# Fifteen row blocks instead of sixteen for the experts of a mixture-of-experts stage, with pieces of 32, 64 and 128 rows

## The chip, the cores and the metric

The kernel runs on one core of one Trainium2 chip. The metric is the device time of one execution in microseconds (us). The time before is 2076.75 us, the median of three runs (2075.97 to 2078.27 us).

## The reference, cut to what matters

Two layers are computed for 640 tokens of width 1024. Each layer has three mixers that read one input projection, and then a channel mixer: a mixture of 16 experts, of which each token takes two. Only that last part is touched here.

```python
def moe_ffn(h, w_router, router_bias, wg, wu, wd):
    scores = jax.nn.sigmoid(xt @ w_router)
    ...                                    # best group, then its best two experts: eidx (T, 2)
    e_flat = eidx.reshape(-1)              # 640 tokens x 2 = 1280 rows, each for one of 16 experts
    ...                                    # the rows are sorted by expert and padded
    def expert_block(args):
        xblk, e = args
        a = jax.nn.silu(xblk @ wg[e]) * (xblk @ wu[e])     # (rows, 1024) @ (1024, 512), twice
        return a @ wd[e]                                   # (rows, 512) @ (512, 1024)
    ...                                    # each token's two rows are weighted and added
```

Everything is float32. The weights of one expert are three matrices of 2 MB each (gate, up and down), so a layer reads 48 of them.

## The kernel before

**Rows and blocks.** In each layer the kernel counts on the chip how many rows each expert has, and ranks the experts by that count. Rank 0 is the fullest. Each rank has a fixed capacity of rows (`CAPS`) and a fixed first row (`BASES`) in a list of rows that is cut into blocks of 128. With capacities of 256, 256, 192, 192, six times 128 and six times 64 there are `NBK` = 16 blocks. An expert with more rows than its rank's capacity sends the rest to one of `OVB` = 8 overflow blocks, which are computed behind the others, in a loop whose body is skipped where there is nothing to do.

**The order of the blocks.** `RUN` names for each step the block and the two ranks that own its lower and upper 64 rows: four blocks belong to two ranks, twelve to one. `MATS` is the order in which the weights are fetched. For each step in which ranks are new it lists their gate, then their up, then their down matrices. `LAST` is the last step that uses a rank.

**Weights.** There are `NSLOT` = 8 slots of 2 MB in SBUF. Matrix m goes to slot m modulo 8, and the sync engine (SP) issues its fetch (line 449) once matrix m - 8 has been used for the last time (`moe_used`, awaited at line 355). SP issues them strictly in the order of `MATS`. Behind the last of them, SP issues the first three weight blocks of the next layer's input projection.

**One step on TensorE.** The loop is:

```python
for i in range(NBK):
    pe.wait_ge(xT_evac, nth(l, NBK, i + 1))
    hidden(i, 0)              # gate product, 8 k-steps
    if i + 1 < NBK:
        tokens_in(i + 1)      # transposes of the next block's tokens (L843)
    hidden(i, 1)              # up product, 8 k-steps
    if i:
        outputs(i - 1)        # down products of the block before, 2 halves of 4 k-steps
    turn_hidden(i)            # four transposes (L866)
```

All gate, up and down products are made by `product` (line 855). For each k-step and each piece of the block it issues one matmul: the piece's rows of the transposed tokens are the stationary operand (128 x rows), 512 columns of the expert's weights are streamed, and the result goes to the piece's rows of a PSUM bank. The profile has two records for each such float32 matmul, here called two passes. A block of one rank has one piece with 128 columns of TensorE's array. A block of two ranks has two pieces with 64 columns each, which lie beside each other in the array.

**Around it.** GpSimd gathers each block's tokens from DRAM (line 1287). VectorE copies the transposed tokens, multiplies gate and up, and copies one half of the result. ScalarE does the activation, copies the other half, and stores each finished block of results in DRAM.

Of the kernel before, what the change touches and what calls it, by code (L numbers as in the profile page):

```python
# [28 lines left out]
P = 128  # L29
# [30 lines left out]
NE = 16  # L60
# [2 lines left out]

CAPS = [256, 256, 192, 192] + [128] * 6 + [64] * 6
BASES = [sum(CAPS[:i]) for i in range(NE)]
NBK = sum(CAPS) // P
NB = NBK + OVB


RUN = [(7, (4, 4)), (0, (0, 0)), (1, (0, 0)), (13, (10, 11)), (2, (1, 1)), (3, (1, 1)), (14, (12, 13)), (4, (2, 2)),
       (5, (2, 3)), (6, (3, 3)), (15, (14, 15)), (8, (5, 5)), (9, (6, 6)), (10, (7, 7)), (11, (8, 8)), (12, (9, 9))]
NSLOT = 8


def moe_matrices():

    order, last = [], {}
    for i, (_, who) in enumerate(RUN):  # L80
        new = [s for s in sorted(set(who)) if s not in last]
        order += [(s, j) for j in range(3) for s in new]
        for s in who:
            last[s] = i
    return order, last


MATS, LAST = moe_matrices()
MAT = {m: i for i, m in enumerate(MATS)}
NEG = 1e30  # L90
# [27 lines left out]
def nth(l, per, n):  # L118
    return l * per + n
# [12 lines left out]
def build_program(nc, A):  # L132
    with ExitStack() as ctx:
# [3 lines left out]
        def sem(name):  # L137
            return ctx.enter_context(nc.semaphore(name))

        def dram(name, shape):  # L140
            return nc.dram_tensor(name, shape, F32, kind="Internal").ap()
# [5 lines left out]
        x_dram = dram("x_dram", [T, D])  # L147
        exp_dram = dram("exp_dram", [NB * P, D])

# [23 lines left out]
        def view(off, n, pattern=None, **kw):  # L173
            v = ar[:, off:off + n]
            return v.rearrange(pattern, **kw) if pattern else v
# [46 lines left out]
        yb = [view(26624 + 1024 * s, 1024) for s in range(2)]  # L222
# [6 lines left out]
        at_row = view(12288, 10 * P, "p (a r) -> p a r", a=10)  # L229
        at_block = view(12288 + 10 * P, 10 * NB, "p (a b) -> p a b", a=10)  # L230

        def slotA(j):
            return wA[:, j * SLOT:(j + 1) * SLOT]
# [8 lines left out]
        def bank(i, n=512):  # L242
            return psum[:, i * 512:i * 512 + n]
# [9 lines left out]
        def sm(n):  # L253
            o[0] += n
            return small[:, o[0] - n:o[0]]
# [23 lines left out]
        rowf, blkf = sm(10), sm(10)  # L279
        ids = ismall[:, 10:10 + NB]  # L280
        novi = ismall[:, 36:37]
# [53 lines left out]
        xg_in = [sem("xg_in0"), sem("xg_in1")]  # L335
        xT_done, xT_evac = sem("xT_done"), sem("xT_evac")
        gate_done, up_done, sg_ready, a_ready = sem("gate_done"), sem("up_done"), sem("sg_ready"), sem("a_ready")
        aT_done, aT_ready, y_done = sem("aT_done"), sem("aT_ready"), sem("y_done")
        yA_evac, yB_evac = sem("yA_evac"), sem("yB_evac")
        y_stored = [sem("y_stored0"), sem("y_stored1")]  # L340
# [10 lines left out]
        def until(eng, signal, n):  # L351


            eng.wait_ge(signal, n)
            eng.sem_inc(passed[eng.engine], 1)
# [19 lines left out]
        def moe_landed(l, m):  # L375

            s_, n = m % NSLOT, m // NSLOT + 1
            return (landedA[s_], loadsA(l, s_, (3, 2, 4)[s_]) + 16 * n) if s_ < 3 else (landedB[s_ - 3], l * 96 + 16 * n)

        def moe_used(l, m):  # L380

            s_, j = MATS[m]
            return (gate_done, up_done, y_done)[j], (32 if j == 2 else 16) * l + (LAST[s_] + 1) * (2 if j == 2 else 1)

        def s3(v, k=KD):
            return v.rearrange("p (k c) -> p k c", k=k)
# [107 lines left out]
        def _(pe):  # L494
# [19 lines left out]
            for l in range(DEPTH):  # L514
# [103 lines left out]
                for ci, c in enumerate(JOBS):  # L618
# [21 lines left out]
                    for j in range(NL + 1):  # L640
# [11 lines left out]
                        for w in range(NT):  # L652
                            tk = slice(w * P, (w + 1) * P)
                            for h in range(2):
                                r = slice(64 * h, 64 * h + 64)
# [19 lines left out]
                    if dr == 1:  # L675
# [12 lines left out]
                        for w in range(NT):  # L688
                            ent = (0 if w == 0 else 1 + w, 1 if w == 0 else 2 + w)
                            for d_ in range(2):  # L690
                                for h in range(2):
                                    r = slice(64 * h, 64 * h + 64)
# [114 lines left out]
                for t in range(NT):  # L807
                    pe.wait_ge(tr_evac, nth(l, N_TR, 2 * NT + 2 * t + 2))
                    for half in range(2):
# [3 lines left out]
                        w = s3(slotA(SLOT_OF[7 + half]))  # L813
# [14 lines left out]
                for a in range(2 * NT):  # L828
                    mm = pe.matmul(bank(5)[:, 0:NB], at_row[:, a, :], at_block[:, a, :],
                                   start=a == 0, stop=a == 2 * NT - 1)  # L830
# [3 lines left out]
                def tokens_in(i):  # L834

                    p = i % 2
                    pe.wait_ge(xg_in[p], l * 128 + 16 * (i // 2 + 1))
                    if i:
                        pe.wait_ge(xT_evac, nth(l, NBK, i))
                    if i >= 2:  # L840
                        pe.wait_ge(aT_ready, nth(l, NBK, i - 1))
                    for k in range(KD):
                        mm = pe.transpose(psum[:, 3072 + k * P:3072 + (k + 1) * P], xg[p][:, k * P:(k + 1) * P], ident)  # L843
                    mm.then_inc(xT_done, 1)

                def product(out, act_T, i, j, kn, cs):

                    a, b = RUN[i][1]
                    parts = [(a, slice(0, P))] if a == b else [(a, slice(0, 64)), (b, slice(64, P))]
                    for s_, r in parts:  # L850
                        pe.wait_ge(*moe_landed(l, MAT[s_, j]))
                    for k in range(kn):
                        for s_, r in parts:
                            w = s3(moe_slots[MAT[s_, j] % NSLOT], kn)
                            mm = pe.matmul(out[r, :], act_T[:, k, r], w[:, k, cs], start=k == 0, stop=k == kn - 1)  # L855
                    return mm
# [4 lines left out]
                def turn_hidden(i):  # L861
                    pe.wait_ge(a_ready, nth(l, NBK, i + 1))
                    if i + 1 < NBK:
                        pe.wait_ge(xT_evac, nth(l, NBK, i + 2))
                    for q in range(4):
# [64 lines left out]
        def _(act):  # L930
# [18 lines left out]
            for l in range(DEPTH):  # L949
# [45 lines left out]
                for b, dst, fn in ((1, kf, ACT.Sigmoid), (2, qf, ACT.Copy)):  # L995
# [4 lines left out]
                    for c in (range(5) if b == 1 else (0, 4)):  # L1000
                        pb = unit_ready(AT[b, c])
                        if c < 4:
                            a = act.activation(dst[:, c, P:T], pb, fn)
                        else:
                            a = act.activation(dst[:, :, 0:P], pb.rearrange("p (c t) -> p c t", c=4), fn)
# [20 lines left out]
                for ci, c in enumerate(JOBS):  # L1026
                    at = {second: n for n, first, second in UNITS[ci]}
# [9 lines left out]
                    for j in range(NL):  # L1037
# [4 lines left out]
                        if j == 1:  # L1042
# [4 lines left out]
                            a, b = (kfac, qfac) if c < 2 else (qfac, kfac)  # L1047
# [94 lines left out]
                def y_half(i):  # L1142
                    act.wait_ge(y_done, nth(l, 2 * NBK, 2 * i + 2))
                    if i >= 2:
                        act.wait_ge(y_stored[i % 2], l * 128 + 16 * (i // 2))
                    act.activation(yb[i % 2][:, W:D], bank(5), ACT.Copy).then_inc(yB_evac, 1)  # L1146

                def y_store(i):
                    act.wait_ge(yA_evac, nth(l, NBK, i + 1))
                    act.wait_ge(yB_evac, nth(l, NBK, i + 1))  # L1150
                    act.dma_start(exp_dram[RUN[i][0] * P:(RUN[i][0] + 1) * P, :], yb[i % 2]).then_inc(y_stored[i % 2], 16)

                for i in range(NBK):
                    act.wait_ge(gate_done, nth(l, NBK, i + 1))
# [11 lines left out]
                y_half(NBK - 1)  # L1166
                y_store(NBK - 1)

                until(act, y_stored[0], l * 128 + 128)
                until(act, pos_ready, l + 1)  # L1170
                nov = act.value_load(novi[0:1, :], min_val=0, max_val=OVB)
                with act.Fori(0, OVB) as j:
# [17 lines left out]
                for t in range(NT):  # L1190
                    for q in range(2):
                        a = act.activation(by_weight[:, 2 * t + q, :], ident, ACT.Copy, scale=wt[:, t, q:q + 1])
# [8 lines left out]
        def _(gp):  # L1201
            gp.memset(condW[:], 0.0).then_inc(cond_zero, 1)
            gp.memset(mhalf, -0.5)
            for s_ in range(NE):
                gp.memset(table[:, 0, s_:s_ + 1], float(CAPS[s_]))
                gp.memset(table[:, 1, s_:s_ + 1], float(BASES[s_]))
            gp.memset(zeros, 0.0)
# [6 lines left out]
            for l in range(DEPTH):  # L1214
# [66 lines left out]
                until(gp, h_stored[0], l * 48 + 48)  # L1281
                until(gp, h_stored[1], l * 32 + 32)
                until(gp, ids_ready, l + 1)
                for i, (blk, _) in enumerate(RUN):
                    if i >= 2:
                        until(gp, xT_done, nth(l, NBK, i - 1))
                    gp.indirect_dma_start(xg[i % 2], None, tok_dram,  # L1287
                                          bass.IndirectOffsetOnAxis(ap=ids[:, blk:blk + 1], axis=0)).then_inc(xg_in[i % 2], 16)
                until(gp, pos_ready, l + 1)
                until(gp, xT_done, nth(l, NBK, NBK))  # L1290
                nov = gp.value_load(novi[0:1, :], min_val=0, max_val=OVB)
# [10 lines left out]
                        gp.dma_start(spare[0:1, bass.ds(j, 1)], bass.AP(A["router_bias"].tensor, 0, [[1, 1], [1, 1]])).then_inc(ov_g, 16)  # L1302
                until(gp, ov_g, l * (16 * OVB) + 16 * OVB)

                until(gp, y_stored[0], l * 128 + 128)
                until(gp, y_stored[1], l * 128 + 128)
                until(gp, ov_st, l * (16 * OVB) + nov * 16 + 16)

                for t in range(NT):
# [15 lines left out]
        def _(v):  # L1325
# [64 lines left out]
            for l in range(DEPTH):  # L1390
# [355 lines left out]
                for t in range(NT):  # L1746
                    dr_()
                    a = tt(before[:, (t + 1) * NE:(t + 2) * NE], before[:, t * NE:(t + 1) * NE], M[:, t, :], ALU.add)
# [52 lines left out]
                for q, oh in enumerate((oh1, oh2)):  # L1801
# [12 lines left out]
                dr_()  # L1814
                tt(at_block, blkf.unsqueeze(2).to_broadcast([P, 2 * NT, NB]),
                   cst[:, C_IOTA:C_IOTA + NB].unsqueeze(1).to_broadcast([P, 2 * NT, NB]), ALU.is_equal)
                tt(at_row, rowf.unsqueeze(2).to_broadcast([P, 2 * NT, P]),
# [33 lines left out]
                def y_half(i):  # L1851
                    v.wait_ge(y_done, nth(l, 2 * NBK, 2 * i + 1))
                    if i >= 2:
                        v.wait_ge(y_stored[i % 2], l * 128 + 16 * (i // 2))
                    v.tensor_copy(yb[i % 2][:, 0:W], bank(4)).then_inc(yA_evac, 1)

                tokens_out(0)
# [121 lines left out]
```

## Time and profile before

| | |
|---|---|
| median of three runs | 2076.75 us |
| profiled execution | 2085.36 us |
| its span | 2083.5 us |
| busy: TensorE, its weight loads, VectorE, ScalarE, GpSimd | 1809.4, 927.7, 755.3, 374.4, 310.7 us |
| mean granted TensorE clock | 0.936 of full speed |
| DRAM traffic over the span | 182 GB/s |

The profile is of one execution. PE is TensorE's matmul stream and PEld its weight loads, DVE is VectorE, ACT ScalarE, POOL GpSimd and SP the sync engine. L855 is line 855 of the kernel. Matmuls overlap, so the duration of one (592 ns) is longer than the distance from its start to the next one's.

### The profile page before, as it was taken

The numbers are of one execution on the slowest core, as the hardware profiler recorded it, in microseconds if no ns is written. First come the engines' busy times: TensorE is split into PE (matmuls) and PEld (weight loads), VectorE is DVE, ScalarE is ACT, GpSimd is POOL, SyncE is SP. The second block draws the span as 40 slices with busy tenths as digits, with TensorE's granted clock in tenths as the row PEclk, the third lists the DMA queues.
The fourth block names the chain that finished last, engine by engine and source line by source line (L and its number), as shares of the span: only waits on it lengthen the run. The fifth ranks groups of instructions, "written<-read, shape, count | busy, mean of one in ns | idle before, by whom it ended". The sixth has DMA issues, their size and how long they took to land. (4 is left out here: it accounts for less than half of the span.)

```text
span 2083.5 us, 20602 instructions
## 1 busy us (share of the span) xinstructions
PE 1809.4 (87%) x7528; PEld 927.7 (45%) x7528; DVE 755.3 (36%) x1179; ACT 374.4 (18%) x695; POOL 310.7 (15%) x348
## 2 busy tenths in 40 slices
PE   3999999788956999999799999988798399999983
PEld 1464555554443443434345445554545243443431
DVE  0036567374462110111060575746636310110105
ACT  1323122243010000000141422213411000000002
POOL 0001266000000000000130223630000000000005
PEclk9999999899977999999899999998998599999996
DMA  9421111565019687799603012136121696797934
GB/s 364 151 98 41 36 54 46 207 238 194 21 51 364 251 328 291 286 358 379 220 38 125 13 46 84 47 132 222 54 75 42 249 348 233 294 357 299 393 124 151
DMA packets 142086, 380.43 MB, mean 183 GB/s; under 512 B 9732, under 2 KB 15876, under 8 KB 135332
## 3 DMA queue, kind: packets, MB, share of 16 engines
q1 hardware_dynamic: 111840, 292.31, 37.5%
q10 hardware_dynamic: 21108, 55.36, 7.5%
q0 software_dynamic: 9040, 31.46, 4.1%
q8 instruction: 61, 1.00, 0.2%
q14 instruction: 37, 0.30, 0.0%
HBM read 343.65 MB, written 35.45 MB: 182 GB/s over the span
## 5 line engine op out<-in xcount | busy, mean ns | idle before, releaser
L855 PE MATMUL psum<-sb_arena 128*128 128x512 f32 (+1 forms) x1248 | 494.1, 596 | 10.6 <-DMA sb_arena<-w_up 9.1
L583 PE MATMUL psum<-sb_wA,sb_arena 128*128 128x512 f32 x800 | 365.3, 605 | 0.9 <-DMA sb_wA<-w_in 0.9
L855 PEld LDWEIGHTS psum<-sb_arena 128*128 128x128 f32 (+1 forms) x1248 | 192.5, 171 | 269.7 <-issue 257.7
L855 PE MATMUL psum<-sb_wA,sb_arena 128*128 128x512 f32 (+1 forms) x672 | 278.4, 611 | 9.3 <-DMA sb_wA<-w_up 6.6
L583 PEld LDWEIGHTS psum<-sb_wA,sb_arena 128*128 128x128 f32 x800 | 147.5, 192 | 165.3 <-issue 158.0
L1329 DVE TENSOR_TENSOR sb_arena<-sb_arena 128x320 f32<-128x320 f32 (+8 forms) x252 | 170.8, 719 | 13.4 <-POOL sb_arena L1264 3.8
L1849 DVE COPY sb_arena<-psum 128x1024 f32<-128x1024 f32 x32 | 39.2, 1225 | 344.3 <-PE psum L843 344.3
L855 PEld LDWEIGHTS psum<-sb_wA,sb_arena 128*128 128x128 f32 (+1 forms) x672 | 103.3, 170 | 120.2 <-issue 109.7
L1495 DVE COPY_PREDICATED sb_arena<-sb_masks,psum 128x640 f32<-128x640 uint8 x128 | 112.4, 878 | 90.8 <-PE psum L656 71.5
L574 PE MATMUL psum<-sb_arena,sb_wA 128*128 128x128 f32 (+1 forms) x512 | 140.4, 435 | 0.0
L815 PE MATMUL psum<-sb_wA,sb_arena 128*128 128x512 f32 x320 | 140.3, 599 | 0.0
L1287 POOL DMA_INDIRECT sb_arena<-tok_dram,sb_ismall x32 | 30.3, 946 | 654.1 <-PE psum L843 539.6
L1329 DVE TENSOR_TENSOR sb_arena<-sb_arena,psum 128x512 f32<-128x512 f32 x38 | 26.1, 687 | 272.3 <-PE psum L855 227.7
L1264 POOL TENSOR_TENSOR sb_arena<-sb_arena 128x640 f32<-128x640 f32 x56 | 80.7, 1444 | 287.4 <-ACT sb_arena L1039 251.5
L656 PEld LDWEIGHTS psum<-sb_arena 64*128 64x128 f32 x1280 | 79.4, 193 | 62.8 <-issue 56.1
L656 PE MATMUL psum<-sb_arena 64*128 64x128 f32 x1280 | 91.6, 287 | 14.9 <-DVE sb_arena L1495 12.7
L574 PEld LDWEIGHTS psum<-sb_arena,sb_wA 128*128 128x128 f32 x512 | 77.0, 191 | 60.0 <-issue 59.3
L1146 ACT ACTIVATE sb_arena<-psum 128x512 f32<-128x512 f32 x32 | 19.1, 597 | 461.4 <-PE psum L855 461.4
L1217 POOL TENSOR_TENSOR sb_small<-sb_small 128x4 f32<-128x4 f32 (+3 forms) x24 | 27.5, 1146 | 448.3 <-DVEq L1615 220.1
L815 PEld LDWEIGHTS psum<-sb_wA,sb_arena 128*128 128x128 f32 x320 | 60.9, 192 | 74.8 <-issue 74.8
L1329 DVE TENSOR_TENSOR sb_arena<-psum,sb_gate_mod 128x512 f32<-128x512 f32 (+1 forms) x30 | 26.1, 870 | 133.6 <-PE psum L815 87.8
L1155 ACT ACTIVATE sb_arena<-psum 128x512 f32<-128x512 f32 x32 | 19.2, 599 | 284.2 <-PE psum L855 284.2
(184 smaller groups left out, 1685.1 us busy)
## 6 DMA issues: line engine op xcount, KB each, us to landing
sb_arena<-w_gate SPq DMA_DIRECT2D x22, 2048.0 KB, 18.5
sb_arena<-w_down SPq DMA_DIRECT2D x22, 2048.0 KB, 15.8
sb_wA<-w_up SPq DMA_DIRECT2D x16, 2048.0 KB, 19.4
sb_arena<-w_up SPq DMA_DIRECT2D x16, 2048.0 KB, 15.5
sb_wA<-w_ada SPq DMA_DIRECT2D x13, 2048.0 KB, 7.7
sb_wA<-w_in SPq DMA_DIRECT2D x12, 2048.0 KB, 9.6
sb_arena<-w_ada SPq DMA_DIRECT2D x11, 2048.0 KB, 7.6
sb_wA<-w_gate SPq DMA_DIRECT2D x10, 2048.0 KB, 18.0
```

What stands on the lines that cost most here:

```text
L574: mm = pe.matmul(out, w[:, k, cc_ * P:(cc_ + 1) * P], hT[:, k, tok], start=k == 0, stop=k == KD - 1)
L583: mm = pe.matmul(unit_bank(n), hT[:, k, t * P:(t + 1) * P], w[:, k, :], start=k == 0, stop=k == KD - 1)
L656: mm = pe.matmul(U(h)[:, tk], ks[r, tk], qs[r, tk], start=True, stop=True)
L815: mm = pe.matmul(bank(n % 3), hT[:, k, t * P:(t + 1) * P], w[:, k, :], start=k == 0, stop=k == KD - 1)
L855: mm = pe.matmul(out[r, :], act_T[:, k, r], w[:, k, cs], start=k == 0, stop=k == kn - 1)
L1155: act.activation(sg[i % 2], bank(2 * (i % 2)), ACT.Silu).then_inc(sg_ready, 1)
L1217: gp.tensor_tensor(dst, src, mhalf[:, 0:dst.shape[1]], ALU.pow).then_inc(rstd_ready, 1)
L1264: gp.tensor_tensor(Kb[:, j % 2], kf[:, c], Eb[:, (j - 1) % 2], ALU.mult).then_inc(K_ready, 1)
L1287: gp.indirect_dma_start(xg[i % 2], None, tok_dram, bass.IndirectOffsetOnAxis(ap=ids[:, blk:blk + 1], axis=0)).then_inc(xg_in[i % 2], 16)
L1329: return v.tensor_tensor(out, a, b, op)
L1495: v.copy_predicated(w5(ATT[:, dr, h, :]), mk, w5(psum[:, (3 + 2 * h) * 512:(3 + 2 * h) * 512 + T])).then_inc(lv_acc, 1)
L1849: v.tensor_copy(xgT[i % 2], psum[:, 3072:4096].rearrange("p (k t) -> p k t", k=KD)).then_inc(xT_evac, 1)
```

## The change

The capacities become 256, 224, 192, 192, 128, seven times 96 and four times 64, which is 1920 rows, or 15 blocks. The ranks no longer stand in the list in their own order but in that of `ROWS`, and the blocks are computed in the order in which they lie. A rank may begin and end at any multiple of 32 rows, so its rows can lie in two neighbouring blocks. `block_parts` cuts each block into pieces of 128, 64 or 32 rows, each aligned to its size. In order, the blocks consist of:

| block | pieces: rank (rows) |
|---|---|
| 0, 4, 10 | 11 (64, 32), 14 (32); 10 (64, 32), 13 (32); 6 (64, 32), 12 (32) |
| 1, 5, 11 | 14 (32), 5 (32, 64); 13 (32), 9 (32, 64); 12 (32), 8 (32, 64) |
| 2 and 3; 6; 7; 9; 12 | one piece of 128 each: 0; 4; 3; 2; 1 |
| 8 | 3 (64), 2 (64) |
| 13, 14 | 1 (64, 32), 15 (32); 15 (32), 7 (32, 64) |

So eight blocks have three pieces, one of 64 and two of 32; one block has two of 64; six have one of 128. The counts that semaphores are compared with follow from the new number of blocks, of which 8 use the first of each pair of buffers and 7 the second.

```diff
-CAPS = [256, 256, 192, 192] + [128] * 6 + [64] * 6
-BASES = [sum(CAPS[:i]) for i in range(NE)]
+CAPS = [256, 224, 192, 192, 128] + [96] * 7 + [64] * 4
+ROWS = (11, 14, 5, 0, 10, 13, 9, 4, 3, 2, 6, 12, 8, 1, 15, 7)
+BASES = [sum(CAPS[r] for r in ROWS[:ROWS.index(s)]) for s in range(NE)]
 NBK = sum(CAPS) // P
+PAIR = [(NBK + 1) // 2, NBK // 2]
 NB = NBK + OVB
-RUN = [(7, (4, 4)), (0, (0, 0)), (1, (0, 0)), (13, (10, 11)), (2, (1, 1)), (3, (1, 1)), (14, (12, 13)), (4, (2, 2)),
-       (5, (2, 3)), (6, (3, 3)), (15, (14, 15)), (8, (5, 5)), (9, (6, 6)), (10, (7, 7)), (11, (8, 8)), (12, (9, 9))]
+def block_parts(i):
+
+    parts = []
+    for s in ROWS:
+        at, end = max(BASES[s], i * P) - i * P, min(BASES[s] + CAPS[s], i * P + P) - i * P
+        while at < end:
+            w = next(w for w in (P, 64, 32) if at % w == 0 and at + w <= end)
+            parts.append((s, slice(at, at + w)))
+            at += w
+    return parts
+
+
+RUN = [block_parts(i) for i in range(NBK)]
 NSLOT = 8
...
-    for i, (_, who) in enumerate(RUN):
-        new = [s for s in sorted(set(who)) if s not in last]
+    for i, parts in enumerate(RUN):
+        who = sorted({s for s, _ in parts})
+        new = [s for s in who if s not in last]
...
-                    a, b = RUN[i][1]
-                    parts = [(a, slice(0, P))] if a == b else [(a, slice(0, 64)), (b, slice(64, P))]
-                    for s_, r in parts:
+                    for s_ in sorted({s_ for s_, _ in RUN[i]}):
                         pe.wait_ge(*moe_landed(l, MAT[s_, j]))
                     for k in range(kn):
-                        for s_, r in parts:
+                        for s_, r in RUN[i]:
                             w = s3(moe_slots[MAT[s_, j] % NSLOT], kn)
                             mm = pe.matmul(out[r, :], act_T[:, k, r], w[:, k, cs], start=k == 0, stop=k == kn - 1)
...
-                    act.dma_start(exp_dram[RUN[i][0] * P:(RUN[i][0] + 1) * P, :], yb[i % 2]).then_inc(y_stored[i % 2], 16)
+                    act.dma_start(exp_dram[i * P:(i + 1) * P, :], yb[i % 2]).then_inc(y_stored[i % 2], 16)
```

## Rows read from the trace of the kernel before

**Rows 1.** The page: busy us of each engine in the whole span.

```profile
span 2083.5 us, 20602 instructions
PE 1809.4 (87%) x7528; PEld 927.7 (45%) x7528; DVE 755.3 (36%) x1179; ACT 374.4 (18%) x695; POOL 310.7 (15%) x348
```

**Rows 2.** Busy time of each engine in the two expert stages.

```profile
650.50:1022.40 371.90, 362.12 (x1144) 157.00 (x1144) 40.44 (x47) 26.82 (x47) 16.77 (x22) 0.98 0.84 312
1657.30:2026.00 368.70, 359.67 (x1144) 156.08 (x1144) 40.45 (x47) 26.85 (x48) 16.80 (x22) 0.99 0.79 298
```

**Rows 3.** Chain of waits, second layer's expert stage: start, us, what.

```profile
1657.28 10.04 PE psum L855 x16
...
1743.26 9.49 DMA sb_arena<-w_up
1752.79 14.15 PE psum L855 x48
...
1904.59 10.22 DMA sb_wA<-w_up
1914.85 15.85 PE psum L855 x48
1931.29 6.87 PE psum L855 x16
...
1953.20 6.87 PE psum L855 x16
```

**Rows 4.** Waits of TensorE in each expert stage, second layer's first.

```profile
PE psum L855 <- DMA sb_arena<-w_up: 4.6, 2, 2.4
PE psum L855 <- DMA sb_wA<-w_up: 2.9, 1, 2.9
...
PE psum L855 <- DMA sb_arena<-w_up: 4.5, 2, 2.4
PE psum L855 <- DMA sb_wA<-w_up: 3.7, 1, 3.7
```

**Rows 5.** Timeline of SP, then DMA issues with us to landing.

```profile
1658.57 6.87 SPq L449 DMA_DIRECT2D sb_arena<-w_gate  x2
...
1743.26 0.37 SPq L449 DMA_DIRECT2D sb_arena<-w_up  x1
...
sb_arena<-w_gate SPq DMA_DIRECT2D x1, 2048.0 KB, 21.4
...
sb_arena<-w_up SPq DMA_DIRECT2D x1, 2048.0 KB, 9.5
```

**Rows 6.** Timeline of TensorE, whole blocks and a block of two pieces.

```profile
1676.33 7.03 PE L855 MATMUL psum<-sb_arena 128*128 128x512 f32 x16
1683.20 1.04 PE L843 MATMUL psum<-sb_cst,sb_arena 128*128 128x128 f32 x8
1684.08 7.03 PE L855 MATMUL psum<-sb_arena 128*128 128x512 f32 x16
...
1720.26 7.09 PE L855 MATMUL psum<-sb_arena 128*64 128x512 f32 x32
1727.28 1.09 PE L843 MATMUL psum<-sb_cst,sb_arena 128*128 128x128 f32 x8
1728.30 7.09 PE L855 MATMUL psum<-sb_wA,sb_arena 128*64 128x512 f32 x32
```

**Rows 7.** Timeline of TensorE, records of a product of two pieces.

```profile
1789.38 0.64 PE L855 MATMUL psum<-sb_wA,sb_arena 128*64 128x512 f32 x1
1789.86 0.59 PE L855 MATMUL psum<-sb_arena 128*64 128x512 f32 x1
1789.86 0.59 PE L855 MATMUL psum<-sb_wA,sb_arena 128*64 128x512 f32 x1
1790.29 0.59 PE L855 MATMUL psum<-sb_arena 128*64 128x512 f32 x1
```

**Rows 8.** Timeline of TensorE, one k-step with four pieces of 32.

```profile
411.84 0.39 PE L751 MATMUL psum<-sb_arena 128*128 128x128 f32 x2
412.16 1.06 PE L502 MATMUL psum<-sb_arena,sb_condW 128*32 128x512 f32 x8
413.15 1.45 PE L738 MATMUL psum<-sb_arena 64*128 64x128 f32 x8
```

**Rows 9.** Timeline, first layer's end and the next layer's first weights.

```profile
994.22 5.45 SPq L421 DMA_DIRECT2D sb_wA<-w_in  x1
...
1015.29 7.13 PE L855 MATMUL psum<-sb_arena 128*128 128x512 f32 x16 [0.74 <-ACT sb_arena L1163]
...
1052.84 7.03 PE L583 MATMUL psum<-sb_wA,sb_arena 128*128 128x512 f32 x16
```

More of the change, by code:

```diff
@@ L382, in moe_used @@
             s_, j = MATS[m]
-            return (gate_done, up_done, y_done)[j], (32 if j == 2 else 16) * l + (LAST[s_] + 1) * (2 if j == 2 else 1)
+            return (gate_done, up_done, y_done)[j], (l * NBK + LAST[s_] + 1) * (2 if j == 2 else 1)
         def s3(v, k=KD):
@@ L836, in tokens_in @@
                     p = i % 2
-                    pe.wait_ge(xg_in[p], l * 128 + 16 * (i // 2 + 1))
+                    pe.wait_ge(xg_in[p], 16 * (l * PAIR[p] + i // 2 + 1))
                     if i:
@@ L1144, in y_half @@
                     if i >= 2:
-                        act.wait_ge(y_stored[i % 2], l * 128 + 16 * (i // 2))
+                        act.wait_ge(y_stored[i % 2], 16 * (l * PAIR[i % 2] + i // 2))
                     act.activation(yb[i % 2][:, W:D], bank(5), ACT.Copy).then_inc(yB_evac, 1)
@@ L1167, in _ @@
                 y_store(NBK - 1)
-                until(act, y_stored[0], l * 128 + 128)
+                until(act, y_stored[0], 16 * (l + 1) * PAIR[0])
                 until(act, pos_ready, l + 1)
@@ L1283, in _ @@
                 until(gp, ids_ready, l + 1)
-                for i, (blk, _) in enumerate(RUN):
+                for i in range(NBK):
                     if i >= 2:
@@ L1287, in _ @@
                     gp.indirect_dma_start(xg[i % 2], None, tok_dram,
-                                          bass.IndirectOffsetOnAxis(ap=ids[:, blk:blk + 1], axis=0)).then_inc(xg_in[i % 2], 16)
+                                          bass.IndirectOffsetOnAxis(ap=ids[:, i:i + 1], axis=0)).then_inc(xg_in[i % 2], 16)
                 until(gp, pos_ready, l + 1)
@@ L1303, in _ @@
                 until(gp, ov_g, l * (16 * OVB) + 16 * OVB)
-                until(gp, y_stored[0], l * 128 + 128)
-                until(gp, y_stored[1], l * 128 + 128)
+                until(gp, y_stored[0], 16 * (l + 1) * PAIR[0])
+                until(gp, y_stored[1], 16 * (l + 1) * PAIR[1])
                 until(gp, ov_st, l * (16 * OVB) + nov * 16 + 16)
@@ L1853, in y_half @@
                     if i >= 2:
-                        v.wait_ge(y_stored[i % 2], l * 128 + 16 * (i // 2))
+                        v.wait_ge(y_stored[i % 2], 16 * (l * PAIR[i % 2] + i // 2))
                     v.tensor_copy(yb[i % 2][:, 0:W], bank(4)).then_inc(yA_evac, 1)
```

## The prediction, as it was put on record

> **What bounds the kernel now.** I read the page first: TensorE is busy for 87% of the span, no other engine for more than 36% [rows 1]. The change touches only the expert stages, so I cut the span into stretches. They last 371.9 and 368.7 us, TensorE is busy for 362.1 and 359.7 us of them, VectorE for about 40 and ScalarE for 27 [rows 2]. The reader is to see there that TensorE has hardly a gap, and that both layers hold the same 1144 matmul records. The chain of waits of the second layer says the same: it is made of L855's matmuls, and now and then of a fetch of an up matrix [rows 3]. What these fetches cost is read from TensorE's own waits, 4.6 + 2.9 us in the second layer and 4.5 + 3.7 in the first, 15.7 us in all [rows 4]. So time in these stages is the number and length of TensorE's products, plus a little waiting for weights.
>
> **One block.** From 1931.29 to 1953.20, one undisturbed step takes 21.9 us [rows 3]. It holds 24 k-steps: 8 for gate, 8 for up, 8 for down. A product of 8 k-steps takes 6.87 us from its start to that of the next instructions (1676.33 to 1683.20) [rows 6], which is 0.859 us a k-step, 0.429 a pass.
>
> **The block that goes.** 16 blocks become 15 in each of two layers: -2 x 21.9 = -43.8 us. Its gather, copies and store on the other engines go too, and lie beside TensorE's work anyway.
>
> **Pieces of one width.** A product of two pieces of 64 columns takes 7.02 us (1720.26 to 1727.28), only 0.15 more than a whole one, though it has twice the matmuls [rows 6]: its records start two at a time, and the next two 0.43 us later [rows 7]. So pieces of equal width that lie beside each other run together. Four pieces of 32 do as well: a k-step of eight records lasts from 412.16 to 413.15, which is 0.99 us [rows 8], and 0.86 of it is the two passes. The 0.13 to 0.15 us that remain come with every change of the array's shape: the four-piece step changes from 128\*128 to 128\*32 and on to 64\*128; the product of two pieces changes in and out as well, and its first pair of records is followed after 0.48 instead of 0.43 us [rows 7]; the transposes between two such products take 1.02 us (1727.28 to 1728.30) instead of 0.88 (1683.20 to 1684.08) [rows 6]. I take 0.14 us for each stretch between two changes of shape.
>
> Before, 4 blocks x 3 products = 12 products a layer have two pieces, after, 3: -9 x 0.15 x 2 = -2.7 us.
>
> **Pieces of unlike width.** This is the step that decides. Eight of the fifteen blocks have, in each k-step, one piece of 64 columns and two of 32. The trace of before has no k-step that mixes widths, so its cost has to be bounded. Below: the three run together like the four equal ones, the whole product costs 0.15 us more than a plain one, and a k-step 0.88 us. Above: they don't, and each k-step is several stretches. The nearest row to such a stretch is the four-piece k-step: two passes, entered and left by a change of shape, 0.99 us [rows 8]. If the 64-wide piece (two passes alone) and the two 32-wide ones (two passes together) follow each other, a k-step has two such stretches and costs 1.98 us. I take this value. What speaks for it is that a change of shape is paid in all the rows, be it in columns or in rows of the array, while pieces of one shape start within 0.01 us of each other; so the shape looks like a setting of the whole array, which it can't have in two ways at once. Two more orders are possible. If the passes are interleaved (64, 32s, 64, 32s), there are four changes a k-step: 4 x (0.429 + 0.145) = 2.30 us. If the 32-wide pieces overlap only where one's second pass meets the other's first, there are five passes and two changes: 2.43 us.
>
> The Trainium skill, "TensorEngine Tiling (Array Packing)", section Key Properties, says that changing the tiling mode, and not just the tile, drains the TensorE. By that page the sum is the one with stretches behind each other; the rows show the price of a change, but no overlap or lack of it between unlike pieces.
>
> So a three-piece block costs 24 x 1.98 = 47.5 us in products instead of 24 x 0.859 = 20.6, 26.9 more. Eight blocks, two layers: 16 x 26.9 = +430.5 us. Nothing covers it: TensorE is the bound, and its queue is in order, so all that stands behind a slow product waits.
>
> **The waits for weights.** An isolated refill works like this in the chain [rows 3, 5]: a slot is freed at the end of a step's down product, SP issues at 1743.26, 0.95 us later, and the matrix lands after 9.5 us. TensorE has turn_hidden, the next gate product and the transposes meanwhile, 0.44 + 6.87 + 0.88 = 8.2 us, and waits the 2.3 us that are left, for the up matrix. Going through the new `MATS` with 8 slots, a matrix needed one step after its slot is freed stands at four places: the up of ranks 9, 3, 8 and 15, in blocks 5, 7, 11 and 13. Before there were three such places. In blocks 5, 11 and 13 the gate product has three pieces and takes 16 us, which hides the fetch; in block 7 it doesn't. That leaves 2 x 2.4 = 4.8 us of 15.7: -10.9 us. There is one new early place: block 1 needs a seventh matrix (rank 5's gate). The seventh is issued at 1658.57 and lands 21.4 us later, at 1680.0 [rows 5], when block 1 would start at 1676.3 [rows 6]. It is hidden if block 0 is slow, and costs 3.5 us a layer if it is not.
>
> **The clock.** After the wait at 1914.85 three products took 15.85 instead of 14.15 us [rows 3], so part of them ran at the lower clock level; and the first layer's stage is 3.2 us longer than the second's with the same records [rows 2]. With fewer waits, between 0 and 6 us of this goes: I take -3.
>
> **Next layer's weights.** SP issued them 28 us before the stage ended (994.22 against 1022.4), and they are first used at 1052.84 [rows 9]. Now SP has to wait for rank 1's down product of block 13, made in the last step, about 17 us before the end. Two fetches behind that need some 16 us, and the use is 30 us behind the end: nothing. Vector and Scalar work per block is unchanged. No wait is added that anything is queued behind.
>
> **The sum.** -43.8 + 430.5 - 2.7 - 10.9 - 3 = +370 us. The profiled execution took 2085.4 us, so it would be 2455; it stood 8.6 us above the median of the runs. On that median, 2076.75 + 370 = 2447 us.
>
> **The rivals.**
>
> *Unlike pieces run together (faster).* Then: -43.8 - 2.7, + 24 products x 0.15 x 2 = +7.2, + 2 x 3.5 = +7 for block 1, and 4 refill waits of 2.4 us a layer, 19.2 instead of 15.7, +3.5: -29 us. With one more fall of the clock, 2050 us, between 2040 and 2062. For it: equal pieces overlap perfectly, down to 32 columns, and unlike ones conflict as little, since they use other columns. Against it: the price of every change of shape. It decides at a clear point: (43.8 + 2.7 - 10.5) / 384 three-piece k-steps is 0.094, so the change loses as soon as such a k-step costs over 0.95 us instead of 0.859.
>
> *The same serialisation, but dearer.* Interleaved passes (2.30 us a k-step) add (2.30 - 1.98) x 384 = 123 us: 2570. Five passes (2.43) add 173: 2620. For the first: records of two pieces alternate, first passes first [rows 7]. Against it: the second pass of a lone 64-wide piece is in the queue at once, with no reason to give way.
>
> *An overflow block.* The smaller capacities could send rows to the overflow blocks. The reference's routing of its inputs gives at most 207, 198, 101, 101, 92, 90 rows and so on in the first layer, and 234, 180, 177, 169, 108, 79 in the second, ninth 65 and 35: all fit. Otherwise each costs two serial fetches and four products, above 40 us.
>
> *The weights bound it anyway (no change).* Then a block less gives nothing: 2077. Against it: TensorE waits for weights for 7.5 of 368.7 us [rows 2, 4].
>
> **How the numbers follow.** Stretches one behind the other at 1.98 us: 0.52; its own range is 2415 (0.05 us of a change not paid twice, 1.90 a k-step, -31) to 2460 (0.145 for each change). Interleaved, 2570: 0.18. Five passes, 2620: 0.10. Together, 2050: 0.17. Overflow on top of anything: 0.02. No change: 0.01. The range from 2405 to 2625 holds the three serial cases, 0.80. A measurement of this kernel can tell 0.2% from no change, 4.2 us: faster 0.17, same 0.01, slower 0.82.
>
> **What would show it.** A k-step of three pieces in the timeline of TensorE: two starts 0.43 us apart for the 64-wide piece, then two pairs for the 32-wide ones, and 2.0 us to the next k-step. Three-piece blocks of 47 to 49 us, others of 22. Waits for weights only at block 7. I am wrong if the three pieces start within 0.01 us of each other: then expect three-piece products of 7.0 us, waits at blocks 1, 5, 7, 11 and 13, and a stage near 350 us.

## The result

The changed kernel takes 2441.2 us (median of four runs, 2439.6 to 2446.5), the kernel before 2077.5 in the same comparison. The ratio is 1.1753, with a 95% interval from 1.1735 to 1.1772: slower by 17.5%. The prediction was 2447 us. Of the experiments below, one execution of the run in pieces of 32 (e1) took 5338 us, against 2066 to 2072 for the other five; it left no trace, its cause is open, and the ratio leaves it out.

The two expert stages, from the first gate product to the last down product, by the windows view of the changed kernel (columns as in [rows 2]: stretch, length, busy us of PE, PEld, DVE, ACT and POOL with instruction counts, granted clock, DMA share, GB/s):

```profile
644.50:1197.30 552.80, 548.81 (x1708) 143.40 (x1708) 37.88 (x45) 25.54 (x45) 15.96 (x21) 0.99 0.57 209
1831.90:2381.60 549.70, 545.76 (x1708) 142.69 (x1708) 37.85 (x44) 25.55 (x45) 15.90 (x21) 1.00 0.54 199
```

They last 552.8 and 549.7 us instead of 371.9 and 368.7 [rows 2], together 361.9 us more. The whole span grew by 356.1 us (2439.6 - 2083.5), so all of the loss is here. TensorE is busy for all but 4 us of each stage, at a granted clock of 0.99 and 1.00, and the DMA engines move 209 and 199 GB/s where they moved 312 and 298: the stages are longer because TensorE's own work is, and not because it waits for weights.

What it does is seen in the timeline of TensorE (start, us, line, tiles, array rows\*columns, shape, count), at the first block's up product:

```profile
663.18 1.09 PE L859 MATMUL psum<-sb_cst,sb_arena 128*128 128x128 f32 x8
664.20 1.62 PE L869 MATMUL psum<-sb_wA,sb_arena 128*64 128x512 f32 x3
665.21 0.62 PE L869 MATMUL psum<-sb_arena 128*32 128x512 f32 x1
665.66 0.59 PE L869 MATMUL psum<-sb_wA,sb_arena 128*32 128x512 f32 x1
665.66 0.59 PE L869 MATMUL psum<-sb_arena 128*32 128x512 f32 x1
666.19 1.62 PE L869 MATMUL psum<-sb_wA,sb_arena 128*64 128x512 f32 x3
```

The first row merges the two passes of the 64-wide piece with the first record of a 32-wide one (both stream from the same tile). That record and the row at 665.21 are the first passes of the two 32-wide pieces. Their second passes start together at 665.66. The next k-step begins at 666.19, which is 1.99 us after the last. So the 64-wide piece has the array for itself for two passes, then the two 32-wide ones share it for two passes.

The chain of waits in the second layer (start, us, what) shows whole products, and the one wait for weights that was forecast for block 7:

```profile
1867.58 15.88 PE psum L869 x48
1883.46 1.02 PE psum L859 x8
1884.49 30.76 PE psum L869 x96
1915.84 6.87 PE psum L869 x16
...
2088.67 9.83 DMA sb_wA<-w_up
2098.54 14.00 PE psum L869 x32
```

A product of three pieces takes 15.88 us, a whole one 6.87 as before. (L869 makes the products, L859 the transposes of tokens.) The 30.76 us of 96 records are two products of three pieces, one right behind the other; that they take 1.0 us less than 2 x 15.88 is explained below. Waits of TensorE in the whole span (us in total, times, longest), for L869's weights:

```profile
PE psum L869 <- DMA sb_wA<-w_up: 4.7, 2, 2.4
```

Before there were 15.7 us of these waits [rows 4].

### The profile page after: what moved, and what is told of

It is laid out like the page before. It is cut to its first block and busy times, and to the rows that moved or that the text cites. A ratio compares the mean times of both kernels' runs of the same rounds, so it can differ in the third digit from the quotient of the medians.

```text
span 2439.6 us, 22842 instructions
## 1 busy us (share of the span) xinstructions
PE 2174.8 (89%) x8656; PEld 898.2 (37%) x8656; DVE 749.3 (31%) x1173; ACT 371.2 (15%) x689; POOL 308.5 (13%) x346
## 5 line engine op out<-in xcount | busy, mean ns | idle before, releaser
L869 PE MATMUL psum<-sb_arena 128*32 128x512 f32 (+2 forms) x1856 | 745.4, 606 | 1.4 <-ACT sb_arena L1177 1.4
L869 PE MATMUL psum<-sb_wA,sb_arena 128*32 128x512 f32 (+2 forms) x1216 | 545.6, 611 | 7.3 <-DMA sb_wA<-w_up 4.7
L869 PEld LDWEIGHTS psum<-sb_arena 128*32 128x32 f32 (+2 forms) x1856 | 158.9, 129 | 423.4 <-issue 421.6
L869 PEld LDWEIGHTS psum<-sb_wA,sb_arena 128*32 128x32 f32 (+2 forms) x1216 | 125.5, 137 | 352.0 <-issue 343.3
L1869 DVE COPY sb_arena<-psum 128x512 f32<-128x512 f32 x30 | 20.8, 692 | 166.9 <-PE psum L869 166.9
```

## The experiments

The theory: TensorE's array has one shape at a time. Pieces of equal width run together, a piece of another width waits until they are through, and the change of shape costs 0.14 us more. The rivals are the number of pieces, weight loads or streams in a k-step, a price of changes alone, and the new placement of ranks and order of fetches.

### The same pieces in the kernel before (e4_before_mixed)

```diff
-                    parts = [(a, slice(0, P))] if a == b else [(a, slice(0, 64)), (b, slice(64, P))]
+                    parts = [(a, slice(0, P))] if a == b else [(a, slice(0, 64)), (b, slice(64, 96)), (b, slice(96, P))]
```

> The kernel before with 16 blocks, only that in its four shared blocks the upper 64 rows, which belong to one rank, are cut into two pieces of 32. Same work, same order, same fetches. Theory: its 192 shared k-steps rise from 0.88 to 1.985 us, +213: about 2290. Rival (the loss comes from ranks that lie across blocks, from the order or the fetches): within 5 us of the kernel before, 2077.

Measured: 2300.5 us in one run, 219 above the kernel before on the same chip (2081.2); span 2298.6. The timeline of TensorE has the product of block 3 at the price of the changed kernel, 15.88 us from 715.93 to 731.81, where it was 7.02 [rows 6]:

```profile
715.93 15.95 PE L855 MATMUL psum<-sb_arena 128*64 128x512 f32 x48
731.81 1.09 PE L843 MATMUL psum<-sb_cst,sb_arena 128*128 128x128 f32 x8
```

Nothing else was touched, so cutting one half of a shared block in two is enough for the loss: 24 such products at 8.86 us more are 213 us of the 219. Placement, order and fetches are not its cause.

### All shared blocks in pieces of 32 (e1_all32)

```diff
-            w = next(w for w in (P, 64, 32) if at % w == 0 and at + w <= end)
+            w = P if at == 0 and end >= P else 32
```

> Every block that several ranks share is cut into four pieces of 32; blocks, capacities, order and fetches stay those of the changed kernel. If the array can hold one shape at a time (theory), all pieces of a k-step run together again: a product takes 6.9 to 7.0 us, a shared block 22 us, and the whole about 2050 us (2040 to 2062), with waits for weights at blocks 1, 5, 7, 11 and 13. If it is the number of pieces, of weight loads or of streams in a k-step that costs (rival), four are no better than three: 2440 us or more.

Measured: 2069.2 us, against 2081.2 for the kernel before; ratio 0.9943 (0.9925 to 0.9961). In the chain of waits a product of four pieces takes 7.0 us:

```profile
1836.78 7.00 PE psum L869 x64
1843.78 1.02 PE psum L859 x8
```

The rival falls: with more pieces and more weight loads in a k-step the loss is gone. But the run is 19 us above the 2050 that I expected. Some 4 us of that are the chip's, on which the kernel before took 2081.2 and not 2076.75 us; the gain is 12 us where 27 was forecast. TensorE's waits in the second layer are larger than those counted (us in total, times, longest):

```profile
PE psum L869 <- DMA sb_arena<-w_up: 8.7, 3, 3.9
...
PE psum L869 <- issue: 6.4, 1, 6.4
PE psum L869 <- DMA sb_wA<-w_up: 2.5, 1, 2.5
```

The wait put down to "issue" stands before the gate product of block 1. The chain of waits and the DMA issues show what it is: the seventh matrix, the gate of rank 5, is issued at 1643.35 and needs 24.5 us, to 1667.9. (The row of 6.36 is the wait, the one before it the up product of block 0.)

```profile
1653.15 7.05 PE psum L869 x64
1661.63 6.36 issue
1667.99 9.97 PE psum L869 x64
```

```profile
sb_arena<-w_gate SPq DMA_DIRECT2D x1, 2048.0 KB, 24.5
```

And the product behind the wait takes 9.97 instead of 7.0 us, at a granted clock of 0.71 between 1668 and 1678: it runs partly at the lower clock level.

### Widths one after the other (e2_by_width)

```diff
-                    for k in range(kn):
-                        for s_, r in RUN[i]:
+                    for width in sorted({r.stop - r.start for _, r in RUN[i]}):
+                        for k in range(kn):
+                            for s_, r in RUN[i]:
+                                if r.stop - r.start != width:
+                                    continue
```

> The pieces stay 64, 32 and 32, but a product runs all its k-steps for the 32-wide pieces first and then all for the 64-wide one, so the shape changes twice in a product and not twice in a k-step. Theory (stretches of unlike shape never overlap, and a change costs 0.14 us): a product of three pieces takes 2 x 6.87 + 0.29 = 14.0 us instead of 15.9, 48 such products in both layers save 90 us: about 2350. Rival (unlike pieces could overlap and only the changes are dear): the products fall to 7 us, about 2055.

Measured: 2366.0 us in one run, where 2350 was expected. In the timeline of TensorE the 32-wide half of block 0's up product starts behind the transposes at 666.90, and the 64-wide half at 673.89, 6.99 us later; that half's 16 passes take 7.08 us to the end of the last:

```profile
665.88 1.09 PE L859 MATMUL psum<-sb_cst,sb_arena 128*128 128x128 f32 x8
666.90 0.62 PE L872 MATMUL psum<-sb_wA,sb_arena 128*32 128x512 f32 x1
...
673.89 7.08 PE L872 MATMUL psum<-sb_wA,sb_arena 128*64 128x512 f32 x16
```

With two stretches in a gate or up product instead of sixteen, it takes 14.0 us: two full products' time remains. So of the 9.0 us that a product loses, 6.87 are that unlike widths don't overlap, and the changes of shape are the smaller part, 2.1 us, of which this run saves 1.9. The total saves 75 us and not the 90 expected. The expectation took a down product for one loop of 8 k-steps; it is two of 4, so it has four stretches, and a down and an up product of three pieces take 28.27 us together, not 28.0. That is some 4 us in 16 down products. Another 8 us are gone with the overlap from product to product that the sum below explains. Between 3 and 4 us lie in the chips (the kernel before: 2081.2 here, 2077.5 beside the changed kernel).

### Half as many changes of shape (e6_turned)

```diff
-                        for s_, r in RUN[i]:
+                        for s_, r in (RUN[i][::-1] if k % 2 else RUN[i]):
```

> The changed kernel, with the order of a block's pieces turned round at every second k-step, so that pieces of equal shape meet across neighbouring k-steps: the shape changes once in a k-step and not twice. Theory (0.14 us a change, and two stretches of two passes that never overlap): 8 k-steps take 8 x 1.716 + 9 x 0.14 = 15.0 us instead of 15.9, a k-step about 1.86; 384 k-steps save 43 to 50 us: about 2395. Rival (the price is that of the stretches alone and a change costs nothing there): 2441.

Measured: 2403.0 us in one run, 38 below the changed kernel, where 43 to 50 was expected. The timeline of TensorE repeats every two k-steps, 3.70 us:

```profile
669.34 2.48 PE L869 MATMUL psum<-sb_wA,sb_arena 128*64 128x512 f32 x5
...
673.04 2.48 PE L869 MATMUL psum<-sb_wA,sb_arena 128*64 128x512 f32 x5
```

Eight passes of 0.429 us are 3.43, and two changes share the other 0.27 us, 0.135 each. A product takes 14.94 us (a pair of them 29.88 in the chain of waits), so 48 of them save 45 us, as expected; the 8 us overlap from product to product that the sum below explains is lost here too, which leaves 37.

### Two unlike pieces (e3_two_unlike)

```diff
-                        for s_, r in RUN[i]:
+                        for s_, r in (RUN[i][::2] if len(RUN[i]) == 3 else RUN[i]):
```

> Leaves out the middle piece of every block of three (its rows are not computed), so that a k-step has two pieces, one of 64 and one of 32. Theory: two unlike stretches remain, a k-step still costs 1.98 us, about 2440. Rival (three streams at a time are too many, two are not): 0.88 us a k-step, about 2050.

Measured: 2444.7 us in one run. In the timeline of TensorE the two passes of one piece and then of the other are plain, with 1.98 us from k-step to k-step:

```profile
670.50 1.07 PE L869 MATMUL psum<-sb_wA,sb_arena 128*64 128x512 f32 x2
671.50 1.04 PE L869 MATMUL psum<-sb_arena 128*32 128x512 f32 x2
672.48 1.07 PE L869 MATMUL psum<-sb_wA,sb_arena 128*64 128x512 f32 x2
```

The 32-wide piece alone costs 0.98 us, as much as two of them together in the changed kernel (665.21 to 666.19), and leaving out one of three streams gains nothing.

### A first block with one rank (e5_all32_order)

```diff
-ROWS = (11, 14, 5, 0, 10, 13, 9, 4, 3, 2, 6, 12, 8, 1, 15, 7)
+ROWS = (4, 6, 12, 8, 0, 10, 13, 9, 3, 2, 11, 14, 5, 1, 15, 7)
```

(on top of the run in pieces of 32)

> As the run with all shared blocks in pieces of 32, but the ranks stand in the list as 4, 6, 12, 8, 0, 10, 13, 9, 3, 2, 11, 14, 5, 1, 15, 7, so that the first block has one rank and not two. That run fell 19 us short of 2050. Theory (block 1 waits for the seventh fetched matrix, 6.1 and 6.4 us in the two layers, and the lower clock level after each such wait costs about 3 more): block 1 then needs the fifth matrix at the latest, that wait goes, a shorter one at block 2 comes (about 2 us a layer), about 2055, with 4 refill waits a layer left. Rival (the 19 us lie in the four pieces themselves, or in the refills): 2069 as before.

Measured: 2060.1 us against 2080.7; ratio 0.9899 (0.9881 to 0.9917), an interval that lies below that of e1 (0.9925 to 0.9961). 2055 was expected. The wait at block 1 is gone, but one of 2.4 us at block 2 takes its place, as the chain of waits has it, and four refill waits a layer stay. So block 1's wait was part of the shortfall, and not all of it:

```profile
1664.38 7.00 PE psum L869 x64
...
1687.28 10.00 DMA sb_wA<-w_up
```

### The down matrices fetched later (e7_all32_downs_late, e8_before_downs_late)

Applied to the run in pieces of 32, with the changed kernel's order of ranks, and to the kernel before:

```diff
-    order, last = [], {}
+    order, last, downs = [], {}, []
...
-        order += [(s, j) for j in range(3) for s in new]
+        order += [(s, j) for j in range(2) for s in new] + [(s, 2) for s in downs]
+        downs = new
...
-    return order, last
+    return order + [(s, 2) for s in downs], last
```

> All shared blocks in pieces of 32, the ranks in the order of the changed kernel, and the fetches in another order: the down matrices of a step's new ranks are listed behind the gate and up matrices of the next step's new ranks. No slot that a new up matrix needs is then freed only one step before, and the first block's two downs stand behind block 1's gate and up. Theory (what is left between the run in pieces of 32 and 2050 us are the waits for weights, 6 to 9 us for block 1 and 2 to 4 at four places a layer, and the lower clock level after them): no wait for weights is left, 25 us of waits and some 16 us of low clock go, about 2025 us. Rival (the fetches can't keep up in any order, since the weights arrive at one matrix in 6.2 us): waits return elsewhere, 2055 or more.

> The kernel before with that order of fetches alone, 16 blocks as they were. Theory: its 15.7 us of waits go, and most of the 6 us of low clock behind them: about 2058. The difference of this run to the one with 15 blocks in pieces of 32 and the same order of fetches is then what the packing itself is worth: 43.8 us for two blocks less the 7 us for changes of shape in more shared blocks, 33 to 38 us. Rival (the block that goes gives nothing once the waits are gone): both the same.

Measured: with 15 blocks 2017.7 us against 2079.5, ratio 0.9704 (0.9688 to 0.9720); with 16 blocks 2056.9 us, ratio 0.9901 (0.9884 to 0.9919). 2025 and 2058 were expected. TensorE has no wait for weights in these stages in either. The second layer's stage with 15 blocks, in the windows view:

```profile
1621.50:1960.00 338.50, 335.74 (x2188) 126.61 (x2188) 37.84 (x44) 25.25 (x45) 15.93 (x21) 1.00 0.86 323
```

338.5 us instead of 368.7 [rows 2], at full clock and 323 GB/s instead of 298: the fetches can keep up. The two runs differ by 39.3 us, a little more than the 33 to 38 expected; this is what 15 instead of 16 blocks are worth when TensorE doesn't wait for weights.

## Why the prediction was right

**The bound.** All of the change of time fell into the two expert stages, and TensorE filled them.

**The k-step of unlike pieces.** This was the step that decided. I took 1.98 us, from the four-piece k-step of [rows 8] as the price of one stretch; the changed kernel shows 1.99, and a product 15.88 us where the sum has 15.84. The order is the one taken: two passes of one width, two of the other. Interleaved passes (2.30) and five passes (2.43) did not occur. That equal pieces overlap and unlike ones don't is shown by e1, e2 and e3 together, and e4 has the same price of a product with the placement, order and fetches of before. What the page of the Trainium skill says that the prediction names, "TensorEngine Tiling (Array Packing)", section Key Properties, that a change of the tiling mode drains the engine, agrees with the trace, in which 128\*64 and 128\*32 are modes of their own: a k-step that holds both takes 1.99 us instead of 0.86.

**The changes of shape.** 0.14 us each was taken; e6 gives 0.135.

**The waits.** One refill wait a layer is left, at block 7, 2.35 us in the second layer, 4.7 us in both; 4.8 was forecast. The wait for block 1's gate was hidden by the slow block 0, as said.

**The sum.** 48 products at 15.88 instead of 6.87 us are +432.5. With -43.8, -2.7 and -11.0 for the block, the pieces of 64 and the waits, that makes +375, and the stages grew by 361.9. Two things fill the 13 us between.

The first is missing in the prediction. Four times a layer an up product of three pieces (of block 1, 5, 11 or 14) is followed at once by the down product of the block before. The up product ends with a 64-wide piece in the upper columns, the down product begins with one in the lower, and these two run together. In the timeline of TensorE, where the up product of block 14 (weights in sb_arena) meets the down product of block 13 (in sb_wA):

```profile
2348.34 0.64 PE L869 MATMUL psum<-sb_wA,sb_arena 128*64 128x512 f32 x1
2348.82 0.59 PE L869 MATMUL psum<-sb_arena 128*64 128x512 f32 x1
2348.82 1.14 PE L869 MATMUL psum<-sb_wA,sb_arena 128*64 128x512 f32 x2
```

(The first row's partner is merged into the row ahead of it; the last row also holds the first pass of a 32-wide piece.) Two passes and a change of shape are saved, 1.0 us: a pair takes 30.76 and not 31.76 us. Eight such places are -8.0 us. It is the theory seen once more: pieces of equal width in different columns overlap, even when they belong to different products. In e2 and e6 no such place is left.

The second is the clock, which I had at -3. By the timeline of TensorE, the passes that were followed only after 0.6 us or more, at the lower level, cost 11.9 us beyond their 0.43 each in the two stages before and 6.1 in the changed kernel, -5.8: the first product of block 0, for one, lost 1.4 us in the second layer (17.31 against 15.88), where it had lost 3.2 (10.04 against 6.87). With both, the sum is +361.2. In that term the prediction also misread a row: the 48 records that took 15.85 instead of 14.15 us are two products and not three, an up product in one piece and a down product in two; the term doesn't change by it. The missing overlap and the clock are small beside the 430 us that decided, and both took time off.

**The faster rival's own sum was too good.** Where pieces do run together (e1), the time was 2069 and not 2050, outside the 2040 to 2062 that I gave it. The step at fault is above all the cost of block 1's wait, 3.5 us a layer: it was 6.1 and 6.4 us, and with the lower clock behind it 9.4 in the second layer (6.4 + 9.97 - 7.0). There block 1 could start 18.0 us after the stage's beginning, where before it was 19.0, mainly since block 0's first product took 8.51 and not 10.04 us; and the seventh matrix landed 24.3 us after it and not 22.7. Why it took longer isn't shown. The refill waits were 21.4 us in both layers, where 19.2 was put down. e5, and e7 above all, show that waits and what follows them were the difference: with no wait for weights, the same blocks take 2018 us.

## What to carry to other kernels

When small products are packed beside each other in the array's columns, give all pieces that should overlap the same width, even if that means more pieces: four of 32 cost 7.0 us where 64 + 32 + 32 cost 15.9. If widths must differ, put equal ones next to each other in the order of issue: turning round every second k-step was worth 38 us, and one stretch for each width 75. Before packing rows tighter, look at what a mixed step does in place of a saved one: here one block saved was worth 22 us, and one mixed block cost 27. And a fetch order that is first in, first out over few slots should list each matrix by when it is needed: moving the down matrices behind the next gate and up was worth 1% alone, and 2.4% on top of the packing (ratio 0.9943 to 0.9704).

## What the runs showed of the hardware

A change of the array's shape has two parts. The next pass starts 0.09 us later than it would behind a pass of its own shape (in the changed kernel 665.66 to 666.19, 0.52 to 0.53 us instead of 0.43). And the first pass behind the change is longer, by 0.05 us for a 64-wide piece [rows 7] and by 0.02 for 32-wide ones (665.21 to 665.66). e6 puts the mean of both kinds at 0.135 us in all; what the engine does in it isn't shown. For its two passes, a stretch with one 32-wide piece (e3, 0.98 us) takes as long as one with two (the changed kernel, 0.98), and a k-step of four takes no longer (e1, 7.00 us for eight). Pieces of equal width overlap across products too (2348.82 above). In e1 TensorE stood for 6.4 us before block 1, and the product behind that took 9.97 us instead of 7.0, at a granted clock of 0.71; in the two expert stages of the changed kernel the granted clock was 0.99 and 1.00.
